# Gated linear attention: from a forward sweep with a second, backward pass to one sweep that takes tile i and its mirror tile together

## The reference, cut to what matters

```
def gla_states(k, v, log_a, s0):            # per chunk
    bcum = jnp.cumsum(log_a..., axis=2); b_last = bcum[:, :, -1]
    d_state = einsum('bnchk,bnchv->bnhkv', kc * exp(b_last[:, :, None] - bcum), vc)
    step: S, (decay, ds) -> decay[..., None] * S + ds       # the state BEFORE each chunk is kept
def gla_output(q, k, v, bcum, s_prev):
    qc = q * exp(bcum);  kc = k * exp(-bcum)
    att = where(tril, einsum('bnihk,bnjhk->bnhij', qc, kc), 0)
    o = einsum(att, vc) + einsum('bnihk,bnhkv->bnihv', qc, s_prev)
o_x = gla_scan(forward, from the context's last state) + flip(gla_scan(everything flipped, ...))
y   = rmsnorm(o_x, g) * silu(r)
```

## Time and profile before

| what | us |
|---|---|
| timed executions, median of 3 | 8663.58 (8653.57 to 8666.1) |
| span of the profiled execution | 8670.0 |
| `gla`, start and prologue | 545.0 to 600.4 |
| `gla`, first pass from the first transposes | 600.4 to 789.8 |
| `gla`, second pass to the first load of `mla` | 789.8 to 866.9 |

### The profile page before, as it was taken

How to read it: one execution, slowest core, us unless ns; L and a number is a source line. 1 busy time by engine, 2 the same in 40 slices (tenths; PEclk the granted TensorE clock), 3 DMA queues, 4 the chain that set the end, 5 groups by cost and what they waited for, 6 DMA issues and landing times. The chain is left out here.

```text
span 8670.0 us, 122409 instructions
## 1 busy us (share of the span) xinstructions
PE 8203.3 (95%) x42310; PEld 5969.3 (69%) x42310; DVE 4151.6 (48%) x9069; ACT 1490.4 (17%) x3735; POOL 4185.4 (48%) x4047
## 2 busy tenths in 40 slices
PE   8987899989999999997999999999999999999994
PEld 4446466646777777644777778777777777777773
DVE  2337455533445545554555554455455444444444
ACT  1124332222011111123221110111011011010002
POOL 0011266713666665402666665555555555554434
PEclk9987999999999999998999999999999999999997
DMA  5312588853556563224666666555655555554435
GB/s 228 147 51 65 175 300 298 300 195 130 204 206 221 209 218 136 85 101 161 218 228 230 227 218 212 204 207 194 213 205 195 192 194 178 195 177 164 153 126 219
DMA packets 773878, 1643.34 MB, mean 190 GB/s; under 512 B 37048, under 2 KB 538984, under 8 KB 726972
## 3 DMA queue, kind: packets, MB, share of 16 engines
q1 hardware_dynamic: 717858, 1425.99, 46.6%
q0 software_dynamic: 55584, 211.54, 6.5%
HBM read 1280.61 MB, written 354.70 MB: 189 GB/s over the span
## 5 line engine op out<-in xcount | busy, mean ns | idle before, releaser
L3094 PE MATMUL ex_ps<-ex_xt,land_rows 128*128 x6272 | 959.8, 296 | 34.8 <-issue 34.8
L3094 PEld LDWEIGHTS ex_ps<-ex_xt,land_rows 128*128 128x128 f32 x6272 | 864.0, 192 | 143.3 <-issue 143.1
L3094 PE MATMUL ex_ps<-ex_tx,land_rows 128*128 x6272 | 941.7, 293 | 16.1 <-DVE ex_tmp L3344 16.1
L3397 DVE TENSOR_TENSOR ex_ym<-ex_ps,ex_ym 128x512 f32<-128x512 f32 x1176 | 811.6, 690 | 236.5 <-PE ex_ps L3150 236.5
L3000 POOL TENSOR_TENSOR ex_sa<-ex_a 128x128 f32<-128x128 f32 x182 | 82.7, 454 | 1658.6 <-DVE ex_a L3336 1658.6
L3094 PE MATMUL ex_ps<-ex_tx,ex_sm 128*128 x6272 | 880.3, 294 | 2.3 <-DVE ex_tx L3299 2.3
L3094 PEld LDWEIGHTS ex_ps<-ex_tx,land_rows 128*128 128x128 f32 x6272 | 856.3, 191 | 24.6 <-DVE ex_tmp L3344 22.2
L3094 PEld LDWEIGHTS ex_ps<-ex_tx,ex_sm 128*128 128x128 f32 x6272 | 840.8, 192 | 2.8 <-issue 2.6
L3150 PE MATMUL ex_ps<-land_rows,ex_a 128*128 128x512 f32 x1680 | 784.1, 593 | 0.2
L2985 POOL TENSOR_TENSOR ex_sm<-land_rows 128x512 f32<-128x512 f32 x394 | 500.9, 1271 | 141.0 <-PE ex_ps L3094 118.5
L3209 ACT ACTIVATE ex_tmp<-ex_ps 128x144 f32<-128x144 f32 (+4 forms) x392 | 116.0, 296 | 2503.3 <-PE ex_ps L3094 2502.8
(11 more groups left out here) (465 smaller groups left out, 13427.3 us busy)
## 6 DMA issues: line engine op xcount, KB each, us to landing
land_rows<-in_o_w SPq DMA_DIRECT2D x593, 1024.0 KB, 5.0
land_rows<-wt SPq DMA_DIRECT2D x197, 1024.0 KB, 6.9
ma_cqT<-in_o_w SPq DMA_DIRECT2D x112, 1024.0 KB, 7.3
wt<-ma_bt SPq DMA_DIRECT2D x112, 1024.0 KB, 5.1
de_wr<-in_e_w SPq DMA_DIRECT2D x88, 1024.0 KB, 5.5
xs<-de_zero POOLq DMA_DIRECT2D x136, 512.0 KB, 6.7
ys<-de_zero POOLq DMA_DIRECT2D x136, 512.0 KB, 7.8
en_ch<-in_w_mod SPq DMA_DIRECT2D x48, 1024.0 KB, 5.4
```

The source lines that it names most:

```text
L3094: last = nc.tensor.matmul(PS[:, bank, 0:h], left[:, k], right[k], start=start and k == 0, stop=k == HK - 1, skip_group_check=not start)
L3397: nc.vector.tensor_tensor(out, new, out, ALU.add).then_inc(y_added[t], 1)
```

## The change

Step i takes tile i for the forward direction and its mirror, `tile(i, 1)`, for the backward one: (0, 1) and (1, 0) for the context, then (2, 17), (3, 16), ... (17, 2). All shared instructions stay, with the two directions' halves now of different tiles. So the state of either direction is always at hand when a step needs it: `states` on DVE reads the increments straight out of psS and keeps four states, ACT's `take` is gone, and `inner` adds the product with the states in the same step. A tile's output gets its first half in one step (`keep`, ACT copies it) and its second in another (`add`, DVE), the first eight output steps keep and the last eight add. There is no second pass; r is loaded whole, its Silu is taken four tiles at a time (`open_gates`) and the norm follows the adds (`squares`, `finish`). The z transposes all run ahead (18 in five banks), and EARLY is 6.

```
-            for t in range(NA):
-                if t >= 2: ...
-                sp.dma_start(X[:, t % 2], rows(proj_d[:, COL_Q:COL_V], t)).then_inc(x_in[t % 2], 16)
+            for i in range(NA):
...
+                for d in range(2):
+                    sp.dma_start(X[:, i % 2, d], rows(proj_d[:, COL_Q:COL_V], tile(i, d))).then_inc(x_in[i % 2], 16)
...
+                for d in range(2):
+                    sp.dma_start(V[:, i % 2, d], rows(proj_d[:, COL_V:COL_Z], tile(i, d))).then_inc(v_in[i % 2], 16)
...
             def products(i):
...
-                if t:
-                    pe.wait_ge(ds_out, t)
-                if lat(t - 1):
-                    pe.wait_ge(o_out, lat(t - 1))
+                if i:
+                    pe.wait_ge(state, 2 * i)
+                if lat(i - 1):
+                    pe.wait_ge(o_out, 2 * lat(i - 1))
                 for h in range(HEADS):
                     for c in range(2):
                         r = slice(c * C, (c + 1) * C)
-                        last = nc.tensor.matmul(psS[:, c, h * DV:(h + 1) * DV], ER[r, t % 2, 1, h * P:(h + 1) * P],
-                                                V[r, t % 2, h * DV:(h + 1) * DV], start=True, stop=True)
+                        for d in range(2):
+                            last = nc.tensor.matmul(psS[d * C:(d + 1) * C, c if d == 0 else 1 - c, h * DV:(h + 1) * DV],
+                                                    ER[r, i % 2, 1, h * P + d * C:h * P + (d + 1) * C], V[r, i % 2, d, h * DV:(h + 1) * DV],
+                                                    start=True, stop=True)
             def inner(i):
+                pe.wait_ge(at_out, lat(i))
+                pe.wait_ge(state, 2 * i + 2)
                 for h in range(HEADS):
-                    nc.tensor.matmul(psS[:, 0, ...], AF[:, h], V[:, t % 2, ...], start=True, stop=False)
-                    last = nc.tensor.matmul(psS[:, 0, ...], AB[:, h], V[:, t % 2, ...], start=False, stop=True)
+                    for d, left in enumerate((AF, AB)):
+                        nc.tensor.matmul(psS[:, d, h * DV:(h + 1) * DV], left[:, h], V[:, i % 2, d, h * DV:(h + 1) * DV],
+                                         start=h == 0, stop=False, skip_group_check=True)
+                for h in range(HEADS):
+                    for c in range(2):
+                        for d in range(2):
+                            r = slice(d * C, (d + 1) * C)
+                            before = 2 * i + (c if d == 0 else 1 - c)
+                            last = nc.tensor.matmul(psS[c * C:(c + 1) * C, d, h * DV:(h + 1) * DV], QT[r, i % 2, h, c * C:(c + 1) * C],
+                                                    S[r, before % 4, h], start=False, stop=True, skip_group_check=True)
                 last.then_inc(o_done, 1)
...
-            def take(t):
-                act.wait_ge(ds_done, t + 1)
-                nc.scalar.activation(S[0:C, 2 * t:2 * t + 2]..., psS[0:C, :], ACT.Copy)
-                nc.scalar.activation(S[C:P, b:b + 2]..., psS[C:P, :], ACT.Copy).then_inc(ds_out, 1)
+            def keep(i):
+                act.wait_ge(o_done, lat(i))
+                for d in range(2):
+                    nc.scalar.activation(O[:, tile(i, d) - NC], psS[:, d], ACT.Copy).then_inc(o_out, 1)
...
+            def states(i):                                    # DVE
+                dve.wait_ge(ds_done, i + 1)
+                dve.wait_ge(ed_done, i + 1)
...
+                    for h in range(HEADS):
+                        last = nc.vector.scalar_tensor_tensor(S[:, (n + 1) % 4, h], S[:, n % 4, h], ED[:, i % 2, h, c:c + 1],
+                                                              psS[:, c, h * DV:(h + 1) * DV], ALU.mult, ALU.add)
+                    last.then_inc(state, 1)
+            def add(i):
+                dve.wait_ge(o_done, lat(i))
+                for d in range(2):
+                    o = O[:, tile(i, d) - NC]
+                    nc.vector.tensor_tensor(o, o, psS[:, d], ALU.add).then_inc(o_out, 1)
```

More of the change, by code:

```diff
@@ L1665, in _ @@
+            for k, t in enumerate(last_tiles):
+                sp.wait_ge(mixed, k + 1)
+                sp.dma_start(rows(mix_d[:, 0:W], t), O[:, t]).then_inc(stored, 16)
             sp.wait_ge(stored, 16 * NT)
@@ L1780, in _ @@
[L1780 to L1792 removed]
+            for i in range(EARLY):
+                gates(i)
@@ L1794, in _ @@
+            pe.wait_ge(const_in, 64)
+            pe.wait_ge(z_out, NZ)
+            row_sums(0)
+            decays(0)
+            for i in range(NA):
+                transposes(i)
+                if i + 1 < NA:
+                    row_sums(i + 1)
+                products(i)
+                if i + 1 < NA:
+                    decays(i + 1)
+                if i + EARLY < NA:
+                    gates(i + EARLY)
+                inner(i)
         @block.scalar
@@ new lines, in decay, with open_gates @@
+            def decay(i):
+                act.wait_ge(d_done, i + 1)
+                if i >= 2:
+                    act.wait_ge(state, 2 * i - 2)
+                nc.scalar.activation(ED[:, i % 2].rearrange("p h c -> p (h c)"), psD[:, 0:2 * HEADS], ACT.Exp).then_inc(ed_done, 1)
+            def keep(i):
+                act.wait_ge(o_done, lat(i))
+                for d in range(2):
+                    nc.scalar.activation(O[:, tile(i, d) - NC], psS[:, d], ACT.Copy).then_inc(o_out, 1)
+            def open_gates(g):
+                act.wait_ge(r_in[g], 16 * RB)
+                nc.scalar.activation(R[:, g * RB:(g + 1) * RB], R[:, g * RB:(g + 1) * RB], ACT.Silu).then_inc(silu, 1)
@@ L1910, in _ @@
+            for g, tiles in enumerate(z_banks):
+                bank = (psT[:, 0], psT[:, 1], psS[:, 0], psS[:, 1], psD)[g]
+                dve.wait_ge(z_done, g + 1)
+                nc.vector.tensor_copy(ZT[0:2 * RANK, 4 * g * P:(4 * g + len(tiles)) * P], bank[0:2 * RANK, 0:len(tiles) * P]).then_inc(z_out, 1)
+                if g == 0:
+                    gates(0)
+                    gates(1)
+            gates(2)
             log_alpha(0)
-            take_low_rank(1)
-            for t in range(GT, EARLY):
-                gates(t)
+            for i in range(GT, EARLY):
+                gates(i)
```

440 lines of the change are left out of this document (183 added, 257 removed).

## The result

The changed kernel took 8607.1 us (median of 4, 8606.6 to 8612.4) against 8664.8 for the kernel before on the same chip: ratio 0.9936 [0.9922, 0.9950], 57.7 us less. The forecast was 8641, 22 less, with 8612 as the lower end. The direction is right, the size is not, and the time is that of the first rival (8606). The profiled execution has a span of 8605.3.

The account below looks back on a forecast made before the run. PE at a mean clock of 0.82 was taken to bound the first pass, DVE the second. Start 602.4 + 16 x 14.1 + 5 + end 11.5 = 844.5 against 866.9, 22 us less: 8641 us, range 8612 to 8678.

Parts of the forecast that it names:

- the first rival: Sweep steps: four quarters in flight (P = 11.9, 57 us less, 8606) or clock staying high (40 to 56 less); chance 0.20.
- the prologue: Start of the stage through two context steps: first transposes at 602.4 instead of 600.4, 2 us more.
- the tail: From PE's last to `mla`'s first load: adds, squares, root and reciprocal, 16 products and handover, 11.5 us.
- The step at the high clock: Chain of one new sweep step with every PE instruction at the high clock: 3.6 + 1.95 + 2.8 + 1.75 + 1.95 = 12.0 us.
- the price of a quarter matmul: Increments and products with the states: 32 instructions each, two in flight, 0.061 each, 1.95 us a set; bounds 0.98 and 3.5.
- The rule weighed in the prediction: Skill's 64 by 64 mode: four independent tiles would make P 2 us shorter, the sum 31 lower; mode changes drain the engine.
- The clock: Every sweep step: slow PE clock lifts P from 12.0 to 14.1 us, between 13.8 (one slow stretch) and 14.5.
- the 5 for adds and `log_alpha`: Last 8 output steps: two adds hold DVE, 0.5 us each, and `log_alpha` stands behind them once; 5 us in all.
- `logs`, Silu and the doubled loads hidden: Sweep: `logs` (4.4 us for three tiles), Silu (about 2 for four) and loads of 1 MB a step add no time.
- PE's wait before L1758: Sweep step: expected under 1 us, released by `states`, in the trace of the changed kernel.
- The second rival: Sweep steps: more waits than counted, P = 15 to 16, 8655 to 8672 us, no measurable change; chance 0.17.
- The third: Sweep steps: slow clock from increments to the wait for `states`; kernel slower, P 17.6 and 8698 us at clock 0.68; chance 0.12.

Follow-up runs that it names:

- pairs: Changed kernel with its quarter matmuls reordered so that only two quarters alternate: 8625.5 us with rows alternating (columns shared), 8633.3 us with columns alternating.
- single quarters: Changed kernel with its quarter matmuls reordered so that the same quarter comes four times in a row: 8657.6 us, ratio 0.9993.
- the fill in the kernel before: Kernel before with the gates' matmul done twice in every first-pass tile, results unused in tiles without gates: 8691.6 us, ratio 1.0030.

## Why the prediction was wrong in size

Stage by its own sum: 844.5 was forecast, 794.7 came. Of the 50 us between, 4 are in the prologue (first transposes at 598.3, not 602.4), 0.2 in the tail (11.3, not 11.5) and 45.5 in the sweep: 185.1 us instead of 16 x 14.1 + 5.

**The step at the high clock** was 12.0 and is 10.62 (709.38 to 720.00). By its terms: transposes to q·k 2.75 for 2.7, q·k 1.09 for 0.89; increments to the start of the states 1.38 for 1.95; states with handover 2.41 for 2.8; att @ v 1.96 for 1.75; products with the states 1.03 for 1.95. Of the 1.4 us too many, 0.92 are in the products and 0.57 in the increments, the two sets priced by quarters; the other terms nearly cancel. **The step that failed is the price of a quarter matmul**: "I take two in flight again and 0.061 each: 1.95". The runs put four in turn at 0.027, and even two in turn at 0.042. The row was of a 64 by 128 shape and was carried over to a 64 by 64 one; the lower bound of 0.98 for the set was nearly the value (0.86). Of the two sets only the products with the states show their full 0.9 on the chain; the increments end ahead of the masks, so that there the masks set the start of the states (the prediction had it the other way round: "the masks end before the increments"). That is why pairs cost 0.8 us a step at the high clock and not twice 0.49.

The rule weighed in the prediction held. The loads show four quarters in 0.86 us and the Trainium skill, TensorEngine Tiling (Array Packing), section Key Properties, says that different tiles run independently: the trace agrees, as it does for the pairs. The drain that the same section gives to a change of mode shows as no more than the 0.17 us of "issue" ahead of L1711 and of the next transposes; no run isolates it.

**The clock** was to cost 2.1 us a step. Over the 10.62 of a step at the high clock the sweep has 15.2 us more, 0.95 a step; 1.5 of it is the wait behind `log_alpha` in the step from 720.00, which leaves about 0.86 a step for the clock. One slow stretch cost 1.6 us in most of the steps that had one (12.2 against 10.6), near the 1.75 that the prediction took. What failed is that the loss was put on every step, and eight of sixteen had none. In the runs with pairs (columns shared) and with single quarters the mean lies as far above the step at the high clock, 12.5 - 11.4 and 14.4 - 13.3, so this term failed by itself.

Of the 45.5 us in the sweep, the chain is 16 x 1.38 = 22, the clock 33.6 - 13.7 = 20, and the remaining 3.5 are of the 5 for adds and `log_alpha`. Of these 1.5 came; the adds cost nothing more, since q·k waits behind the row sums anyway. What the clock obeys is open. In the last steps filling a wait of 2.1 us, or making it shorter, kept it up; the step from 709.38 had the same 2.13 us wait and stayed at the high clock; with pairs the clock fell more often behind shorter waits; and the fill in the kernel before left the clock where it was. Why the old tile runs at 0.82 stays open too.

**The rest of the sum** held: tail, prologue within 4 us, `logs`, Silu and the doubled loads hidden. DVE was not ready for the states: in the step shown the masks end 0.4 us behind the increments, and the states start there. In the sweep no wait of PE is put down to ACT. PE's wait before L1758 was to be under 1 us; it is 1.06 in steps with gates and 2.13 without.

**Outside the stage** the prediction assumed that nothing moves; the experts' stage gave 10 us back, and that rests on a cause that the runs can switch on and off but do not name. Without it the time would have been near 8597, further from the forecast.

The first rival had the mechanism of the quarters right, and its time, 8606, was met in part by luck: it took every step with a slow stretch and so had the stage end near 809 (866.9 - 57.6), 15 us later than it did; the experts' 10 us and the scatter of the executions made up for that. The second rival (8655 to 8672) did not come: PE's waits for the states are 1.06 to 2.13 us where the sum had 0.7, but the cheaper quarters more than paid for them. The third (a slow clock takes the step) had the wrong sign.

## What to carry to other kernels

A price is a price for a shape: before a row is carried to another tile size, count how many regions of the array take turns in the program's order, and write loops so that all of them do; the same 64 instructions cost 1.7, 2.7 or 4.6 us here by loop order alone. Where two engines hand a chain back and forth, follow it through both queues before buying time on one: earlier additions and cheaper decays gave nothing because something else stood in the way. And compare stages, not only totals: an untouched stage moved by 10 us.

## What the runs showed that was not expected

- Quarter matmuls of 128 columns: 0.027, 0.042 and 0.0725 us an instruction with four, two and one quarter in turn, whichever side alternates.
- Decays of two columns: 16 instructions on 64-column halves in 0.55 us, 8 on the full width in 0.97.
- Eight products with an addend (128x128) on VectorE took 2.27 us with the addend in PSUM, whether GpSimd was multiplying or not. With the addend in SBUF they took 2.31 where GpSimd was done and up to 3.66 where its products overlapped with them.
- 24 unused PE instructions made a later, untouched stage of 4467 us shorter by 10, along with 4 fewer packets on an instruction queue and fewer waits of PE that the profile puts down to nothing but issue.
- Twelve tiny matmuls at the low clock cost 5.3 us, 0.44 each.
